# Front results through DRAM, row gathers with a place of their own, dots ranked ahead of the rest, in a hybrid decoder step on one core

## What is computed

```python
qa, ka, va, qi, ki, wi, qr, kr, vr, gr = mixer_inputs(rms_norm(hp, norm_attn_w[l]), pos_p, w_in[l])
att = prompt_dsa(qa, ka, va, qi, ki, wi)            # indexer scores, top 256 keys of each row, attention on these
o_r, s_r = prompt_retention(qr, kr, vr)             # chunks of 128, a running state
mix = jnp.concatenate([att, retention_out(o_r, gr, ret_gn_w[l])], axis=-1)
hp = hp + mix @ w_out[l]
# ffn_residual: 8 heads pick 16 of 128*128 experts each, so 128 rows of u and v for every token
hval = jnp.einsum('thkd,td->thk', u_emb[eid], xb)
coef = gate * jax.nn.gelu(hval, approximate=False)
y = jnp.einsum('thk,thkd->td', coef, v_emb[eid])
```

## Time and profile before

| | us |
|---|---|
| median of 3 runs | 3857.44 |
| the profiled execution | 3870.04 |
| its span in the profile | 3868.2 |
| first expert gather starts | 649.6 |
| last expert gather starts | 3840.6 |

### The profile page before, as it was taken

How to read it: one execution, slowest core, us unless ns; L and a number is a source line. 1 busy time by engine, 2 the same in 40 slices (tenths; PEclk the granted TensorE clock), 3 DMA queues, 4 the chain that set the end, 5 groups by cost and what they waited for, 6 DMA issues and landing times.

```text
span 3868.2 us, 31404 instructions
## 1 busy us (share of the span) xinstructions
PE 3178.7 (82%) x9551; PEld 1543.8 (40%) x9551; DVE 2674.1 (69%) x6543; ACT 993.7 (26%) x2512; POOL 1237.8 (32%) x1084
## 2 busy tenths in 40 slices
PE   5999864988798879887987898689887389879776
PEld 2444253443354325433543453245433144334321
DVE  1222138888868778978888888988856998434655
ACT  1111122152134214421432153115222022311211
POOL 0000001444444434443443344234342124333443
PEclk9999977999999999998999899899999699889999
DMA  4111133999999999999999999889998179988998
GB/s 170 57 66 50 54 116 134 391 417 397 392 404 407 415 370 369 394 399 361 397 400 368 364 385 408 341 341 384 356 394 340 70 297 420 392 338 343 414 421 341
DMA packets 190425, 1245.72 MB, mean 322 GB/s; under 512 B 22704, under 2 KB 27184, under 8 KB 50672
## 3 DMA queue, kind: packets, MB, share of 16 engines
q0 software_dynamic: 155520, 1128.34, 72.4%
q1 hardware_dynamic: 34736, 115.37, 7.9%
HBM read 1220.50 MB, written 22.46 MB: 321 GB/s over the span
## 4 chain that ended last, share of the span: by engine, by line
PE 44%; DMA 26%; DVE 24%; issue 3%; ACT 1%; SPq 1%; POOL 1%; DVEq 0%; ACTq 0%; POOLq 0%
PE yacc L1030 23%; DMA weights<-in_uv,eid 19%; PE bank L857 11%; DVE weights L1484 7%; DVE kv L1346 3%; DVE tiny L1345 3%; PE bank L993 3%; DMA weights<-in_w_out 2%; PE bank L967 2%; DVE weights L1416 1%; DVE weights L1215 1%; DVE weights L1412 1%; DMA kv<-in_cache_ik,gi 1%; POOL weights L1838 1%; ACT diag L1747 1%
## 5 line engine op out<-in xcount | busy, mean ns | idle before, releaser
L1030 PE MATMUL yacc<-weights,diag 128*128 128x512 f32 (+1 forms) x4224 | 2002.5, 624 | 364.7 <-ACT diag L1747 363.4
L1838 POOL DMA_INDIRECT weights<-in_uv,eid x1056 | 1210.5, 1146 | 2578.1 <-PE yacc L1030 1875.8
L1484 DVE CUSTOM_DVE_ANT_0 weights<-weights,xn 128x1024 f32<-128x1024 f32 x1056 | 1290.2, 1224 | 597.5 <-DMA weights<-in_uv,eid 585.8
L1030 PEld LDWEIGHTS yacc<-weights,diag 128*128 128x128 f32 (+1 forms) x4224 | 802.5, 196 | 1453.6 <-issue 909.3
L1747 ACT ACTIVATE diag<-main,coef 128x128 f32<-128x128 f32 x1024 | 356.7, 394 | 1450.8 <-DVE coef L1475 1381.1
L1345 DVE MAX8 tiny<-kv 128x8 f32<-128x384 f32 (+6 forms) x224 | 245.0, 1094 | 3.0
L1755 ACT ACTIVATE gl<-hv 128x2 f32<-128x2 f32 x528 | 107.1, 203 | 530.6 <-DVE hv L1484 529.9
L1346 DVE MATCH_REPLACE8 kv<-tiny,kv 128x384 f32<-128x384 f32 (+6 forms) x224 | 241.6, 1079 | 0.0
L967 PE MATMUL bank<-weights 128*128 128x512 f32 (+1 forms) x288 | 158.4, 687 | 87.0 <-DMA weights<-in_w_out 85.8
L857 PE MATMUL bank<-weights 128*128 128x512 f32 (+3 forms) x560 | 229.6, 572 | 0.0
L857 PE MATMUL bank<-weights,mid 128*128 128x512 f32 (+1 forms) x448 | 183.2, 570 | 0.0
(11 more groups left out here) (240 smaller groups left out, 2309.8 us busy)
## 6 DMA issues: line engine op xcount, KB each, us to landing
weights<-in_w_out SPq DMA_DIRECT2D x72, 512.0 KB, 7.8
weights<-in_uv,eid POOLq DMA_INDIRECT x1056, 9.8
Hb<-h_scratch SPq DMA_DIRECT2D x8, 1700.0 KB, 10.7
weights<-in_w_in SPq DMA_DIRECT2D x6, 2048.0 KB, 18.8
h_scratch<-Hb SPq DMA_DIRECT2D x4, 1700.0 KB, 5.5
h_scratch<-spare SPq DMA_DIRECT2D x4, 1700.0 KB, 5.5
nw<-in_wffn SPq DMA_DIRECT2D x9, 512.0 KB, 6.4
nw<-in_wfin SPq DMA_DIRECT2D x9, 512.0 KB, 14.3
```

The lines of the kernel that those rows point to most:

```text
L1030: mm = nc.tensor.matmul(yacc[0:W, 512 * j:512 * (j + 1)], diag[:, n % 4, 0:W], ring[:, n % RING, D + 512 * j:D + 512 * (j + 1)], start=Fal ...
L1484: ins = V.tensor_tensor_reduce(u, u, xn[:, t % 2, :], 1.0, 0.0, ALU.mult, ALU.add, hv[:, n % RING:n % RING + 1])
L1838: pool.indirect_dma_start(dst, None, table, bass.IndirectOffsetOnAxis(ap=ids, axis=0)).then_inc(s, 16)
```

## The change

Seven things, all by the list and the places in it:

1. `mixT` leaves the front. At the front's end a new step `stash` has SP store the attention half and the retention half of `Hb` in `m_scratch` (two DMAs); the next `load` waits for these (`mix_out`) and no longer for `mixT`. The back begins with `remix`: SP loads the row into `h1`, PE transposes it from there, and only when ACT has the second group out of PSUM does `resid` overwrite `h1` with x.
2. The retention steps leave the front for a stream of their own (`side_steps`), and half of the sample's past logits for another (`past_steps`); the sample's top-k rounds are no longer interleaved with them.
3. Gathers are steps of their own (`fetch`), with their own place in POOL's order, put there as soon as the sums that free the ring place are listed.
4. The gate product and ACT's spread become a step `weigh` of their own, no longer behind the next pair's first dot; it is due 0.75 us after its dot. `drain` goes.
5. Dots and sums get due times of -1e7, ahead of every front and back step. `weigh` does not.
6. `ycopy` is listed when the next tile's `keys` are.
7. PERIOD 400 to 360, LEAD 150 to 100, NEAR 0.4 to 0.1, and the sample's front is due over 1.2 PERIOD.

Every DVE instruction of before is there again, each as often, with the same shapes.

```diff
-PERIOD, LEAD, ROW, LATENCY, NEAR = 400.0, 150.0, 2.62, 3.4, 0.4
+PERIOD, LEAD, LATER, LAST, ROW, LATENCY, NEAR = 360.0, 100.0, 0.0, 1.2, 2.62, 3.4, 0.1
...
-    return steps + [Step("mixT", t, 0, "P", 2.6, 1, 2.4)]
+    return steps + [Step("stash", t, 0, "", 0, 1, 5.0)]
...
-    steps = [Step("resid", t, 0, "", 0, 0, 4.0)]
+    steps = [Step("remix", t, 0, "", 0, 0, 4.0), Step("mixT", t, 0, "P", 2.6, 1, 2.4), Step("resid", t, 0, "", 0, 0, 4.0)]
...
-        if t in chosen and drained == t:
-            at = arrival(t, k)
-            if at is not None:
-                yield "D", at, t * PERIOD + PERIOD * k / units(0), "unit"
-        if drained < t:
-            yield "D", dotted[drained, units(drained) - 1] + 0.8, -1e9, "drain"
+        if due:
+            yield "D", dotted[due[0]] + 0.75, dotted[due[0]] + 0.75, "weigh"
+        if dot in fetched:
+            yield "D", fetched[dot], -1e7, "unit"
+        if fetch[0] <= TILES and arrival(*fetch) is not None:
+            yield "", 0.0, 0.0, "fetch"
...
-            yield "P", weighed[t, k] + 1.0, t * PERIOD + PERIOD * k / units(0), "sums"
+            yield "P", weighed[t, k], -1e7, "sums"
+        if copying and (copying[0][0] == TILES or copying[0][0] + 1 in keyed):
+            yield "", copying[0][1], 0.0, "ycopy"
...
                     else:
-                        copied(sp, ("mixT", t - 1, 1))
+                        sp.wait_ge(mix_out, 32 * t)
                     sp.dma_start(Hb[0:R, :], h_dram[t * P:t * P + R, :]).then_inc(h_in, 16)
...
+                elif what == "stash":
+                    sp.wait_ge(mix_ready, t + 1)
+                    sp.wait_ge(gated, t + 1)
+                    if t == SAMPLE:
+                        sp.wait_ge(att_in, 16 * NB * KVH)
+                    sp.dma_start(m_dram[t * P:t * P + R, 0:512], Hb[0:R, 0:512]).then_inc(mix_out, 16)
+                    sp.dma_start(m_dram[t * P:t * P + R, 512:D], Hb[0:R, GR:GR + 512]).then_inc(mix_out, 16)
+                elif what == "remix":
                     if t:
                         sp.wait_ge(seeded, t)
+                    sp.wait_ge(mix_out, 32 * (t + 1))
+                    sp.dma_start(h1[0:R, :], m_dram[t * P:t * P + R, :]).then_inc(mix_in, 16)
+                elif what == "resid":
+                    filled(sp, ("mixT", t, 1))
                     sp.dma_start(h1[0:R, :], x_of(t)).then_inc(residual_in, 16)
...
                     ins = V.tensor_tensor_reduce(u, u, xn[:, t % 2, :], 1.0, 0.0, ALU.mult, ALU.add, hv[:, n % RING:n % RING + 1])
-                    if k and s == PAIR * k:
-                        weigh_pair(t, k - 1)
                 ins.then_inc(hval_ready, 1)
...
-            def drain(t, part):
-                weigh_pair(t, units(t) - 1)
...
-            steps = {"unit": unit, "sscores": sscores, "slogits": slogits, "svalue": svalue}
+            steps = {"fetch": fetch, "sscores": sscores, "slogits": slogits, "svalue": svalue}
```

## The result

The change made the kernel slower: 4732.18 us (median of 4 runs, 4727.86 to 4737.73) against 3859.93 for the kernel before on the same chip (4 runs), ratio 1.226, 95% interval 1.2235 to 1.228. Forecast were 4330 us and a range of 4110 to 4500. The direction was right, the time lies 232 us above the range.

What follows compares the result with a forecast made beforehand. The stream of 1056 gathers of 1 MB bounds wherever fed; DVE's order makes holes. First gather 649.6 + 8, stream 1734 + 1082, gaps 792, sample 30, handover 20, end 27.6: span 4343, median 4332, said 4330; range 4110 to 4500 us.

Steps and rivals of the forecast that it cites:

- The sixteen gaps: DVE's runs of other work over 12 us between dots, tiles 0 to 6: 746 us of work, 86 of refill.
- The time outside gaps: All of the span but those gaps and their refills, from start to end: 3511 us of 4343.
- Why the gate products starve: On DVE, dots and sums go ahead of everything; late front and back steps are due before gate products, which wait.
- the hand-over: Rows through DRAM: first gather 8 us later, 20 us of transfers, PE's later waits at `mixT` costed at nothing.
- The separate place for gathers: POOL's order changes only around the sample's 24 gathers; expert gathers held back only inside gaps; costed at nothing.
- the `resid` load covered by the `out` steps: In the back, `resid` after `mixT` is covered by eight `out` steps, so no wait was expected.
- the forecast's two: Gaps above 12 us between dots on DVE in the kernel before: 93.4 us, the hole in tile 6, and 13.8.
- tiles 5 to 8 at 2.60 us a slot: Gather stream once these tiles' fronts are done: 416 x 2.60 = 1082 us, between 2.50 and 2.71 a slot.
- its rival's 72 to 100: PE waits 8.1 us before each `mixT`, uncovered by the ring: +72 to +100 us, 4400 to 4430; chance 0.07.
- The slow stream: Rival: all 1056 gathers run at tile 4's 2.94 us a slot, +289 us, 4620 us; chance 0.03.
- The bridge: Rival: rows still in flight at a gap's start hide 20 us of each, 320 in all: 3834 us; chance 0.02.
- the uncut upper end, 4602: Range bound before cutting: 4330 plus 193 for slower pace, 72 for PE's waits and 7 for a late start.

Runs made afterwards that it cites:

- the list with both edits: The change with gate products ranked ahead of everything else on VectorE and row gathers issued at their dots again: 3935.7 us, ratio 1.020 to the kernel before.

## Why the prediction was right in kind and short by 400 us

- **What bounds, and what a gap costs: right.** The sixteen gaps came out at 821 us against 832, and from the first gate product to the next dot most of them took 9 to 15 us, where 12 were forecast. Taking their reason away gave 559 us back of the 560 worked out from the same prices. The time outside gaps fits in sum (3499 us against 3511), with errors of 20 to 30 us on either side.
- **Why the gate products starve: right in the main.** That `weigh` is due by the clock and other steps are late is what counts (559 us); that dots and sums have a rank, which the forecast names beside it, does not (19 us).
- **The step that failed** is in the paragraph on the hand-over: "The separate place for gathers changes POOL's order only around the sample's 24; twice four cache gathers stand in a row and hold expert gathers back, but both lie in gaps." It asks only whether cache gathers hold row gathers back. The order moved the other way too: index-key gathers came to stand six rows later, and PE, ACT and DVE waited for them. PE's eight waits for index keys, up to 15.4 us each, are gone with the order undone. The order cost 188 us in the change and 237 where gate products are in time, and the forecast had it at nothing. The rule to ask what is queued behind a waiting instruction was applied to PE at `mixT` and not to PE at the sample's transposes.
- **The rest of the miss, some 200 us** (4544 with that step undone, against 4332), is only partly settled. In spans it is 197 us: eight unforeseen gaps with 144 us remain there, and 60 us stand outside gaps (3571 against 3511). Of the eight, six end with PE in waits for output weights, for a handed-over row, or in back steps, with the sums behind them; the prediction had the `resid` load covered by the `out` steps and did not ask what the `out` steps wait for. That gaps come from elsewhere than DVE was there to be seen: read like this, the trace of the kernel before has five more than the forecast's two, 13 to 15 us each with at most 7.1 us of DVE work in them, which pricing DVE's list does not find. No run took these waits alone.
- **A term that was too small: tiles 5 to 8 at 2.60 us a slot.** Tile 7, with 16 us of gaps, took 370 us in the change, 2.89 a slot, where 333 were forecast and the bound was 2.71. It had taken as long before (the row below, of the kernel before), and the forecast's 418 GB/s come from 150 us of this same tile. What slows the rest of it was not settled. The reading of the earlier trace rows was too high in the same way: of the 33 slices from the stream's start on, 15 show 390 to 417 GB/s, two more, and 14 show 338 to 385, beside the two holes.

```profile
3392.60:3763.80 371.20, 291.44 (x812) 129.88 (x811) 187.36 (x427) 62.61 (x204) 142.91 (x131) 0.93 0.95 382
```

- **The hand-over.** The first gather was forecast 8 us later and came 1.9 us earlier (647.7 against 649.6), though PE waited 11.7 us for the row, until 526.45. With this one, PE's waits for rows handed over come to 69.6 us in the change. The forecast's nought and its rival's 72 to 100 both stand open for the change itself. In the list with both edits, 115 us more of reading cost 109: there the ring did not cover PE's wait, which the forecast had relied on.
- **The slow stream: wrong as the cause, as forecast.** Slices of 421 and 422 GB/s stand in the row above, and only tile 7 came near the rival's 2.94 us a slot with few gaps. The limit of HBM for one core of about 358 GB/s, as the Trainium skill's page "DMA: Bandwidth & Descriptors" (Specifications) has it, is again passed; the measurement decides.
- **The bridge: wrong.** No row was under way when any of the sixteen gaps began, so the ring hid nothing of them.
- **The range** ended at 4500 because its upper bounds came from known costs (the stream's pace, PE's waits at `mixT`). A part of the change that is costed at nothing had no bound of its own: eight index-key gathers that each hold four engines for some 15 to 20 us would have added 120 to 160. Even the uncut upper end, 4602, lay under the time.

## What to carry to other kernels

When work is taken out of a step and becomes a step of its own, ask what it was safe behind: a due time that follows the real clock loses to any list of steps that is late. When one kind of request gets a new place in a queue, count for every other kind in that queue how far it moved relative to it, in both directions, and follow each late one down to whoever waits for it with work queued behind. And a gap of one engine that is moved to another place in the list costs the same there, unless something that can run is put beside it.

## What was not expected of the hardware

A displacement of six to eight row gathers of 1 MB in POOL's order, some 16 to 22 us of stream at 2.71 us each, nearly doubled the time from one index-key gather to the next (16.6 to 31.2 us). Moving the cache gathers alone gave back 156 us in the change; moving the row gathers alone, 188 to 237. The transfer itself was no slower: 11.2 us in the median from issue to landing in the change, 13.8 with the row gathers at their dots.

In the emptier stretches TensorE's granted clock fell: to 0.75 in the mean over tile 4's stretch, which is half of the time at 1.2 GHz and half at 2.4, against 0.94 before. In the hole shown above it is at 1.2 GHz from 2966.7 on, 3 us after PE began its wait for the keys. PE's busy time rose from 3178.7 to 3234.6 us for the same 9551 matmuls. What the clock itself cost no run separates.
